# A SwiGLU layer with seven half products in place of eight in half of the inner dimension of eight chunks

## The chip, the core and the metric

The kernel runs on one core of one Trainium2 chip. The metric is the device time in microseconds (us) of one execution. The kernel is one program of three transformer blocks for 256 tokens of width 2048; the change is in the feed-forward layer of the first block.

## What is computed

Two things of the reference matter here. The feed-forward layer of the first block has 2048 inputs and 5632 hidden columns, and its result is added to the scaled input and normed:

```python
def swiglu(x, w_gu, w_d):
    gate, up = jnp.split(x @ w_gu, 2, axis=-1)
    return (jax.nn.silu(gate) * up) @ w_d

x = layer_norm(DEEPNORM_ALPHA * x + swiglu(x, ffn_wgu[l], ffn_wd[l]), ln2_g[l], ln2_b[l])
```

All weights and inputs are float32. `x` here has 256 rows, `ffn_wgu[0]` is 2048 x 11264 and `ffn_wd[0]` is 5632 x 2048.

## The kernel before

**Units.** Every large product runs over units of weights: 256 rows by 512 columns (two k-tiles of 128 rows), 128x1024 in memory. A unit goes through four engines. SyncE loads it (`unit_load`) into one of 8 raw slots. ScalarE copies it, rounded, to the high part (`unit_hi`, L217), into one of 4 split slots. VectorE subtracts the high part from the raw weights (`unit_lo`, L230) and so makes the low part in the same slot. TensorE multiplies (`block_mm`, L269 to L271): high by high, low by high and high by low, for 2 k-tiles and 2 halves of the 256 tokens, so 12 matmuls of 512 columns a unit. The counters between them are semaphores: `hi_ready`, `lo_ready` and `w_used` (TensorE has used a unit). ScalarE may write the high part of unit u only when TensorE has used unit u-4, and SyncE may load unit u only when VectorE has split unit u-8.

**Blocks.** 512 output columns for 256 tokens are a block; it takes a pair of the 8 PSUM banks (0 and 1, or 2 and 3, by turns). `evac` takes a block out of PSUM and then frees its pair (`acc_free`); TensorE waits for that before it opens the block after the next.

**The feed-forward layer** (`hidden(0)`) goes over 11 chunks of 512 hidden columns. A step of the loop has 24 units: 8 for the gate block of a chunk, 8 for its up block (all 16 k-tiles of the input), then 4 blocks of 2 units for the down product of the chunk before. After two gate units TensorE turns the hidden values of the chunk before (`turn_hidden`, eight 128x128 transposes a step into banks 4 and 5), and ScalarE and VectorE split these too. ScalarE takes the gate block out with Silu (L1855), VectorE multiplies it with the up block (L2730) and adds each down block to `x` (L1975). The first chunks and the last one are written out; the loop makes 8 trips, for chunks 2 to 9.

**The order of the work** on each engine is fixed by the code: `block_split` puts an evacuation behind the split of the second unit of the next block, so VectorE takes a block out while TensorE works on the two units of the next block, and only behind these does TensorE need the banks. GpSimd has little to do in this layer: at its start it loads vectors and, with `held_load`, four units for the next stage.

## Time and profile before

| | us |
|---|---|
| median of 3 runs | 3443.41 |
| lowest and highest of them | 3443.39, 3445.43 |
| the profiled execution | 3443.67 |
| its span, first to last instruction | 3441.9 |
| TensorE (PE) busy in the span | 3426.8 |
| VectorE (DVE) busy | 1944.3 |
| ScalarE (ACT) busy | 1609.9 |
| GpSimd (POOL) busy | 302.9 |

Some 1.8 us of the profiled execution lie outside its span. Matmuls overlap in the profile: each is shown for about 0.39 us, but the next starts 0.23 us after it. The time of TensorE is therefore read from the starts of matmuls, not from their lengths. The same holds for VectorE and ScalarE: an instruction is shown from start to end, and the next can start shortly before that end.

### The profile page before, as it was taken

The numbers are of one execution on the slowest core, as the hardware profiler recorded it, in microseconds if no ns is written. First come the engines' busy times: TensorE is split into PE (matmuls) and PEld (weight loads), VectorE is DVE, ScalarE is ACT, GpSimd is POOL, SyncE is SP. The second block draws the span as 40 slices with busy tenths as digits, with TensorE's granted clock in tenths as the row PEclk, the third lists the DMA queues.
The fourth block names the chain that finished last, engine by engine and source line by source line (L and its number), as shares of the span: only waits on it lengthen the run. The fifth ranks groups of instructions, "written<-read, shape, count | busy, mean of one in ns | idle before, by whom it ended". The sixth has DMA issues, their size and how long they took to land.

```text
span 3441.9 us, 42740 instructions
## 1 busy us (share of the span) xinstructions
PE 3426.8 (100%) x15844; PEld 2808.4 (82%) x15844; DVE 1944.3 (56%) x2315; ACT 1609.9 (47%) x2063; POOL 302.9 (9%) x418
## 2 busy tenths in 40 slices
PE   9999999999999999999999999999999999999999
PEld 8788878888888888777888878888888788888887
DVE  4544575555555755667556545567544845555546
ACT  5444444444444455454444444446556644444443
POOL 0000010000000000002343303000380000000000
PEclk9999999999999999999999999999999999999999
DMA  7555565556556455456555547655554555655554
GB/s 247 167 169 180 200 205 189 191 183 195 191 186 195 159 172 159 129 195 169 187 188 196 189 159 217 208 194 163 192 173 151 167 187 185 195 185 188 188 186 144
DMA packets 333316, 630.11 MB, mean 183 GB/s; under 512 B 33180, under 2 KB 36096, under 8 KB 331648
## 3 DMA queue, kind: packets, MB, share of 16 engines
q1 hardware_dynamic: 326272, 603.20, 54.7%
q0 software_dynamic: 6768, 25.05, 2.3%
q8 instruction: 86, 1.41, 0.2%
q14 instruction: 46, 0.38, 0.0%
q10 hardware_dynamic: 144, 0.07, 0.0%
HBM read 624.86 MB, written 2.33 MB: 182 GB/s over the span
## 4 chain that ended last, share of the span: by engine, by line
PE 97%; DVE 2%; ACT 1%; issue 0%; DVEq 0%; POOL 0%; ACTq 0%; POOLq 0%
PE psum L269 29%; PE psum L271 28%; PE psum L270 28%; PE psum L323 3%; PE psum L601 1%; PE psum L603 1%; PE psum L602 1%; PE psum L938 1%; PE psum L951 0%; PE psum L3136 0%; PE psum L519 0%; PE psum L517 0%; PE psum L518 0%; DVE weights_lo L230 0%; PE psum L3156 0%
## 5 line engine op out<-in xcount | busy, mean ns | idle before, releaser
L230 DVE TENSOR_TENSOR weights_lo<-weights_raw,weights_hi 128x1024 fp32r<-128x1024 f32 (+1 forms) x1139 | 1398.1, 1237 | 1202.5 <-ACT weights_hi L217 1201.7
L217 ACT CAST weights_hi<-weights_raw 128x1024 fp32r<-128x1024 f32 (+1 forms) x1139 | 1195.0, 1052 | 1656.1 <-PE psum L271 1644.2
L269 PE MATMUL psum<-weights_hi,act_hi 128*128 128x512 f32 x3048 | 1210.9, 397 | 0.1
L271 PE MATMUL psum<-weights_hi,act_lo 128*128 128x512 f32 x3048 | 1189.4, 390 | 0.0
L270 PE MATMUL psum<-weights_lo,act_hi 128*128 128x512 f32 x3048 | 1187.3, 390 | 0.0
L271 PEld LDWEIGHTS psum<-weights_hi,act_lo 128*128 128x128 f32 x3048 | 572.0, 188 | 122.5
L269 PEld LDWEIGHTS psum<-weights_hi,act_hi 128*128 128x128 f32 x3048 | 572.6, 188 | 121.4 <-issue 8.9
L270 PEld LDWEIGHTS psum<-weights_lo,act_hi 128*128 128x128 f32 x3048 | 573.1, 188 | 112.9
L269 PE MATMUL psum<-weights_hi,hid_hi 128*128 128x512 f32 x1320 | 517.4, 392 | 0.0
L271 PE MATMUL psum<-weights_hi,hid_lo 128*128 128x512 f32 x1320 | 514.1, 389 | 0.0
L270 PE MATMUL psum<-weights_lo,hid_hi 128*128 128x512 f32 x1320 | 513.7, 389 | 0.0
L269 PEld LDWEIGHTS psum<-weights_hi,hid_hi 128*128 128x128 f32 x1320 | 247.8, 188 | 53.1 <-issue 2.7
L271 PEld LDWEIGHTS psum<-weights_hi,hid_lo 128*128 128x128 f32 x1320 | 247.7, 188 | 52.0
L270 PEld LDWEIGHTS psum<-weights_lo,hid_hi 128*128 128x128 f32 x1320 | 247.9, 188 | 50.5
L1975 DVE TENSOR_TENSOR x<-x,psum 128x512 f32<-128x512 f32 x170 | 109.1, 683 | 103.0 <-PE psum L271 103.0
L903 POOL DMA_DIRECT2D big<-in_ffn_wgu x8 | 5.8, 724 | 1394.8 <-DVE big L2483 1024.2
L323 PE MATMUL psum<-ident,big 128*128 128x128 f32 (+1 forms) x754 | 117.3, 272 | 0.2 <-DVE hid_lo L340 0.2
L323 PEld LDWEIGHTS psum<-ident,big 128*128 128x128 f32 (+1 forms) x754 | 93.3, 139 | 28.9 <-issue 3.5
L1975 DVE TENSOR_TENSOR big<-big,psum 128x512 f32<-128x512 f32 x56 | 35.9, 683 | 54.6 <-PE psum L271 54.6
L2730 DVE TENSOR_TENSOR big<-big,psum 128x512 f32<-128x512 f32 x44 | 28.3, 685 | 64.6 <-PE psum L271 64.6
L340 DVE TENSOR_TENSOR hid_lo<-psum,hid_hi 128x512 fp32r<-128x512 f32 x76 | 52.0, 684 | 1.3 <-ACT hid_hi L332 1.3
L371 ACT COPY big<-psum 128x512 f32<-128x512 f32 (+5 forms) x113 | 50.7, 449 | 3.9 <-PE psum L3055 3.9
(452 smaller groups left out, 1934.4 us busy)
## 6 DMA issues: line engine op xcount, KB each, us to landing
weights_raw<-in_ffn_wgu SPq DMA_DIRECT2D x344, 512.0 KB, 4.3
weights_raw<-in_w_ff SPq DMA_DIRECT2D x252, 512.0 KB, 3.9
weights_raw<-in_ffn_wd SPq DMA_DIRECT2D x176, 512.0 KB, 3.6
weights_raw<-in_even_w_in SPq DMA_DIRECT2D x120, 512.0 KB, 3.5
weights_raw<-in_w_in SPq DMA_DIRECT2D x64, 512.0 KB, 3.5
weights_raw<-in_odd_w_in SPq DMA_DIRECT2D x60, 512.0 KB, 3.7
weights_raw<-in_odd_w_o SPq DMA_DIRECT2D x32, 512.0 KB, 3.6
weights_raw<-in_w_out SPq DMA_DIRECT2D x32, 512.0 KB, 3.7
```

Source lines behind the costliest of these rows:

```text
L217: nc.scalar.copy(w_hi[:, u % SPLIT_SLOTS, done:size], raw[:, u % RAW_SLOTS, done:size]).then_inc(hi_ready, 1)
L230: nc.vector.tensor_tensor(w_lo[:, u % SPLIT_SLOTS, done:size], raw[:, u % RAW_SLOTS, done:size], w_hi[:, u % SPLIT_SLOTS, done:size].bitca ...
L269: nc.tensor.matmul(o, ah, wh, start=(k + j == 0), stop=False)
L270: nc.tensor.matmul(o, ah, wl, start=False, stop=False)
L271: last = nc.tensor.matmul(o, al, wh, start=False, stop=(k + j == kts - 1))
L323: last = nc.tensor.transpose(psum[:w, 4 + t % 2, at_col:at_col + p], src, ident[:p, :p])
L340: nc.vector.tensor_tensor(dst, psum[:, 4 + t % 2, :], hi.bitcast(F32), ALU.subtract).then_inc(turn_free[t % 2], 1)
L371: nc.scalar.copy(dst, psum[:w, 4 + t % 2, :n]).then_inc(turn_free[t % 2], 1)
L601: nc.tensor.matmul(o, ah, wh, start=(u + j == 0), stop=False)
L602: nc.tensor.matmul(o, ah, wl, start=False, stop=False)
L603: last = nc.tensor.matmul(o, al, wh, start=False, stop=(2 * u + j == KT_D - 1))
L1975: return TENS(o, o, s, ALU.add)
```

## The change

For chunks 2 to 9 the half of the inner dimension in k-tiles 0 to 7 is computed by a scheme of seven products in place of eight. Token halves (2), halves of these 8 k-tiles (2) and gate or up (2) make eight products of 4 k-tiles by 128 tokens by 512 columns. The new code computes seven, P1 to P7, from sums and differences of the token halves' inputs (made once, on GpSimd, `side_sums`) and from sums of the weights (made for each chunk, on VectorE, `weight_sum`). K-tiles 8 to 15 stay as they were (gate 4 to 7 and up 4 to 7). Each P is two half units: a half unit is loaded and split like a unit (128x1024), but has 6 matmuls, not 12.

- A step has 30 splits in place of 24: 8 full gate and up units, 12 half units (P2 to P7), 8 down units, and 2 half units of P1 for the next chunk among the down units. Matmuls of 512 columns a step: 276 in place of 288.
- The weights of the scheme are loaded as quads a, b (raw slots 4 to 7) and c, d (two new buffers), among the down loads; plain units have raw slots 0 to 3. Loaded bytes are the same. Split slots stay 4, and a half unit takes a whole one.
- VectorE adds weights in place in four instructions of 128x2048 a step (for P5, P7, P6, P4), and ScalarE's high part of those units waits for the sums (`summed`).
- Partial results are taken out of banks 6 and 7: four copies on ScalarE (`snap`), and on VectorE `gate_whole` (2 instructions of 128x512), `up_whole` (3) and `hidden_whole` (2) in place of two multiplications. Silu reads SBUF.
- The last instruction of `hidden_whole` frees pair 1, for which TensorE waits before the second down block. The additions of down blocks to `x` stand behind the splits at places 26 and 28 of the step (counted from 0), and 2 and 4 of the next.
- The loop has 3 trips of two steps, with one step written out ahead and one behind.
- `evac` takes both halves of a block in one instruction, everywhere (except for Relu). Some semaphores share a name, with no further effect. `held_load` waits until the last step is nearly through, because its buffers lie where the new operands are.

The core of the diff:

```diff
+ITEMS = [("gate", 4), ("P2", 0), ("P2", 1), ("gate", 5), ("P5", 0), ("P5", 1), ("gate", 6), ("P6", 0), ("P6", 1),
+         ("gate", 7), ("P7", 0), ("P7", 1), ("up", 4), ("P4", 0), ("P4", 1), ("up", 5), ("P3", 0), ("P3", 1),
+         ("up", 6), ("up", 7)]
+DOWN = [("down", 0), ("down", 1), ("down", 2), ("down", 3), ("P1", 0), ("P1", 1),
+        ("down", 4), ("down", 5), ("down", 6), ("down", 7)]
+DOWN_LAST = [item for item in DOWN if item[0] == "down"]
+ITEM = {item: i for i, item in enumerate(ITEMS + DOWN)}
+STEP = len(ITEMS) + len(DOWN)
+SUMS = ["P5", "P7", "P6", "P4"]
+QUAD = {"a": 4, "b": 6, "c": 8, "d": 10}
+PART = {"P1": "a", "P2": "c", "P3": "d", "P4": "a", "P5": "a", "P6": "a", "P7": "b"}
...
+    quad_c, quad_d = (big(o, [P, 2, 2 * UNIT])[:, :, 0:UNIT] for o in (3072, 7168))
+    raw_at = [raw[:, i, :] for i in range(RAW_SLOTS)] + [quad[:, q, :] for quad in (quad_c, quad_d) for q in range(2)]
+    hi_at = [w_hi[:, i, :] for i in range(SPLIT_SLOTS)]
+    lo_at = [w_lo[:, i, :] for i in range(SPLIT_SLOTS)]
...
+    def high_part(act, c, of, size):
+        to = c.split_slot()
+        if to in c.user:
+            act.wait_ge(w_used, c.until(c.user[to] + 1))
...
-    def evac(eng, c, end, block, dst, do):
+    def evac(eng, c, end, block, dst, do, by_half=False):
 
 
         eng.wait_ge(w_used, c.until(end))
         pair = block % 2
-        for m in range(TT):
-            last = do(m, dst(m), psum[:, 2 * pair + m, :])
+        if by_half:
+            for m in range(TT):
+                last = do(m, dst(m), psum[:, 2 * pair + m, :])
+        else:
+            both = slice(0, TT)
+            last = do(both, dst(both), psum[:, 2 * pair:2 * pair + 2, :])
         last.then_inc(acc_free[pair], 1)
...
+            def down(ch, base, next_base):
+                quads = [(x, q) for x in "abdc" for q in range(2)] if next_base is not None else []
+                for u in range(8):
+                    if quads:
+                        quad(*quads[u], ch + 2, next_base)
+                    at = (DOWN if quads else DOWN_LAST).index(("down", u))
+                    slot_load(sp, c, c.raw_slot(), rows(w2, ch * kts + 2 * (u % 2), 2, (u // 2) * BLK), BLK, base + at)
...
+        def side_sums():
+            G = nc.gpsimd
+            halves = [(k, slice(m * P, (m + 1) * P)) for m in range(TT) for k in (slice(0, 4), slice(4, 8))]
+            for to, (k, m) in zip(token_parts, halves):
+                last = G.tensor_tensor(to[:], aT_hi[:, k, m].bitcast(F32), aT_lo[:, k, m].bitcast(F32), ALU.add)
...
+            pool.wait_ge(ready("sides_high"), 2)
+            for p in ("P5", "P6", "P7", "P3"):
+                last = G.tensor_tensor(side_lo[p][:], side_whole[p][:], side_hi[p][:].bitcast(F32), ALU.subtract)
+            last.then_inc(ready("sides_low"), 1)
...
+            def sums_item(item):
+                what, q = item
+                if what in PART:
+                    x = PART[what]
+                    slot = QUAD[x] + q
+                    if what in SUMS:
+                        act.wait_ge(ready("summed"), c.now("summed", SUMS.index(what) + 1))
+                    else:
+                        act.wait_ge(landed[slot], c.now(f"raw{slot}", 1, 1, 16))
+                        c.n[f"raw{slot}"] += 1
+                    if what == "P7":
+                        c.n[f"raw{slot}"] += 1
+                    high_part(act, c, raw_at[slot], UNIT)
+                else:
+                    unit_hi(act, c, UNIT)
...
+                    sums_item(item)
+                    if i == 0:
+                        act.wait_ge(acc_free[(start - 5) % 2], c.freed(start - 5))
+                        snap(r[:, 0, :], 6, base - 4)
+                    if i == ITEM["gate", 4] + 5:
+                        turn_taken(0)
+                    if i == ITEM["gate", 5] + 5:
+                        turn_taken(2)
+                    if i == ITEM["P5", 1] + 5:
+                        snap(up_parts[:, 1, :], 7, base + ITEM["P5", 1] + 1)
+                    if i == ITEM["P6", 1] + 4:
+                        snap(up_parts[:, 0, :], 6, base + ITEM["P6", 1] + 1)
+                    if i == ITEM["P7", 1] + 5:
+                        snap(r[:, 1, :], 6, base + ITEM["P7", 1] + 1)
+                    if i == ITEM["gate", 7] + 7:
+                        gated(0)
+                    if i == ITEM["P4", 1] + 7:
+                        gated(1)
...
+            def weight_sum(what):
+                if what == "P5":
+                    dve.wait_ge(lo_ready, c.now("unit", -1))
+                    landing("b")
+                    ins = TENS(quad_ab, quad_ab, quad_b, ALU.add)
+                elif what == "P7":
+                    dve.wait_ge(ready("summed"), c.now("summed"))
+                    landing("d")
+                    ins = TENS(quad_b, quad_b, quad_d, ALU.add)
+                else:
+                    dve.wait_ge(lo_ready, c.now("unit"))
+                    ins = TENS(quad_ab, quad_ab, quad_d if what == "P6" else quad_c, ALU.add)
+                ins.then_inc(ready("summed"), 1)
+                c.n["summed"] += 1
...
+                def gate_whole(m):
+                    dve.wait_ge(w_used, c.until(base + (ITEM["gate", 7], ITEM["P4", 1])[m] + 1))
+                    if m == 0:
+                        dve.wait_ge(ready("snapped"), c.now("snapped", 1))
+                        TENS(r[:, 0, :], bank(0), r[:, 0, :], ALU.subtract).then_inc(ready("gate_whole"), 1)
+                    else:
+                        dve.wait_ge(ready("snapped"), c.now("snapped", 4))
+                        TENS(r[:, 1, :], bank(1), r[:, 1, :], ALU.subtract).then_inc(acc_free[start % 2], 1)
+                def up_whole():
+                    dve.wait_ge(w_used, c.until(base + ITEM["up", 7] + 1))
+                    dve.wait_ge(ready("snapped"), c.now("snapped", 3))
+                    TENS(up_parts[:, 1, :], bank(2), up_parts[:, 1, :], ALU.add).then_inc(dve_step, 1)
+                    TENS(up_parts[:, 0, :], bank(7), up_parts[:, 0, :], ALU.add).then_inc(dve_step, 1)
+                    dve.wait_ge(dve_step, c.now("dve_step", 1))
+                    TENS(up_parts[:, 1, :], bank(6), up_parts[:, 1, :], ALU.add).then_inc(dve_step, 1)
+                def hidden_whole():
+                    for m in range(TT):
+                        dve.wait_ge(dve_step, c.now("dve_step", 2 + m))
+                        dve.wait_ge(ready("gated"), c.now("gated", m + 1))
+                        ins = TENS(h[:, m, :], r[:, m, :], up_parts[:, m, :], ALU.mult)
+                    ins.then_inc(acc_free[(start + 1) % 2], 1)
...
+                    if item in (("P5", 1), ("P6", 1)):
+                        weight_sum("P6" if item[0] == "P5" else "P4")
+                    if not last and i == ITEM["P1", 1] + 1:
+                        weight_sum("P5")
+                    if i == 2 and before is None:
+                        add_at(base - 2, start - 2, 2)
+                    if i == 4:
+                        if before is None:
+                            add_at(base, start - 1, 3)
+                        else:
+                            before()
+                    if i == ITEM["gate", 4] + 6:
+                        turn_taken(0)
+                    if i == ITEM["gate", 5] + 6:
+                        turn_taken(2)
+                    if i == ITEM["gate", 7] + 5:
+                        gate_whole(0)
+                    if i == ITEM["P4", 1] + 5:
+                        gate_whole(1)
+                    if i == ITEM["up", 7] + 4:
+                        up_whole()
+                    if i == ITEM["up", 7] + 5:
+                        hidden_whole()
+                    if i == ITEM["down", 1] + 5:
+                        add_at(base + ITEM["down", 1] + 1, start + 2, 0)
+                    if not last and i == ITEM["P1", 1] + 2:
+                        weight_sum("P7")
+                    if not last and i == ITEM["down", 3] + 5:
+                        add_at(base + ITEM["down", 3] + 1, start + 3, 1)
+                if last:
+                    add_at(base + ITEM["down", 3] + 1, start + 3, 1)
+                    add_at(base + len(items) - 2, start + 4, 2)
...
+            into = {"P1": 6, "P6": 6, "P7": 6, "P5": 7, "P3": 7, "P2": 0, "P4": 1}
+            behind_snap = {("P6", 0): 1, ("up", 4): 2, ("P7", 0): 3}
...
+            def sums_item(item):
+                what, q = item
+                s = c.split_slot()
+                pe.wait_ge(lo_ready, c.now("unit", 1))
+                for j in range(2):
+                    wh, wl = (w[s][:, j * BLK:(j + 1) * BLK] for w in (hi_at, lo_at))
+                    if what in into:
+                        hi, lo, k0, m = sides[what]
+                        parts = [(hi[:, k0 + 2 * q + j, m], lo[:, k0 + 2 * q + j, m], into[what])]
+                    else:
+                        parts = [(aT_hi[:, 2 * q + j, m * P:(m + 1) * P], aT_lo[:, 2 * q + j, m * P:(m + 1) * P],
+                                  ((0, 1) if what == "gate" else (7, 2))[m]) for m in range(TT)]
+                    for ah, al, b in parts:
+                        start_ = j == 0 and opens[b] == item
+                        stop = j == 1 and b in closes.get(item, ())
+                        nc.tensor.matmul(bank(b), ah, wh, start=start_, stop=False, skip_group_check=True)
+                        nc.tensor.matmul(bank(b), ah, wl, start=False, stop=False, skip_group_check=True)
+                        last = nc.tensor.matmul(bank(b), al, wh, start=False, stop=stop, skip_group_check=True)
+                last.then_inc(w_used, 1)
...
+            def sums_down(last=False):
+                pe.wait_ge(turn_free[0], c.now("turn", 1, 2))
+                pe.wait_ge(turn_free[1], c.now("turn", 0, 2))
+                for j in range(4):
+                    if j == 2 and not last:
+                        for q in range(2):
+                            sums_item(("P1", q))
+                    block_mm(pe, c, kts, BLK, hT_hi, hT_lo)
+            def sums_step(last=False):
+                start = c.n["block"]
+                for i, item in enumerate(ITEMS):
+                    if item == ("gate", 4):
+                        pe.wait_ge(acc_free[start % 2], c.freed(start - 2))
+                    if item == ("up", 4):
+                        pe.wait_ge(acc_free[(start + 1) % 2], c.freed(start - 1))
+                    if item in behind_snap:
+                        pe.wait_ge(ready("snapped"), c.now("snapped", behind_snap[item]))
+                    sums_item(item)
+                    if item == ("gate", 4):
+                        hidden_stands(start - 5, 0)
+                        turn_hidden(0)
+                    if item == ("gate", 5):
+                        turn_hidden(2)
+                c.n["block"] += 2
+                c.n["snapped"] += 4
+                sums_down(last)
```

**Where instructions stand.** First VectorE in the middle of the down product, written out ahead of the loop. `weights_lo` is the low part of a unit; `x<-x,psum` adds a down block; `big` are the gate, up and hidden values. Before, chunk 1:

```order
L2730 TENSOR_TENSOR big_196<-big_194,psum 128x512 [waits w_used,acc_free0]
L2730 TENSOR_TENSOR big_196<-big_194,psum 128x512
L230 TENSOR_TENSOR weights_lo<-weights_raw,weights_hi 128x1024 [waits hi_ready] x2
L1976 SCALAR_TENSOR_TENSOR x<-x,psum 128x512 [waits w_used]
L1976 SCALAR_TENSOR_TENSOR x<-x,psum 128x512
```

and now the first step of the scheme, from behind the split of down unit 3:

```order
L3056 TENSOR_TENSOR big_218<-psum,big_218 128x512 [waits soft_then_snapped,w_used]
L3057 TENSOR_TENSOR big_218<-psum,big_218 128x512
L3059 TENSOR_TENSOR big_218<-psum,big_218 128x512 [waits dve_step]
L301 TENSOR_TENSOR weights_lo<-weights_raw,weights_hi 128x1024 [waits hi_ready]
L3065 TENSOR_TENSOR big_198<-big_196,big_218 128x512 [waits rms_then_gated,dve_step] x2
L301 TENSOR_TENSOR weights_lo<-weights_raw,weights_hi 128x1024 [waits hi_ready] x2
L3025 TENSOR_TENSOR weights_raw<-weights_raw 128x2048 [waits unit_landed7,unit_landed6,lo_ready]
L3042 TENSOR_TENSOR x<-x,psum 128x2x512 [waits w_used]
L301 TENSOR_TENSOR weights_lo<-weights_raw,weights_hi 128x1024 [waits hi_ready]
L3029 TENSOR_TENSOR weights_raw<-weights_raw,big_60 128x2048 [waits unit_landed11,unit_landed10,end_then_summed]
```

The two multiplications that made the hidden values have become three additions, a split and two multiplications, and a sum of 128x2048 stands between a split and the addition to `x` that frees a pair of banks.

Second, VectorE at the top of a step, as the last step has it (written out, without the loop's register instructions). Before:

```order
L230 TENSOR_TENSOR weights_lo<-weights_raw,weights_hi 128x1024 [waits hi_ready] x4
L1975 TENSOR_TENSOR x<-x,psum 128x512 [waits w_used]
L1975 TENSOR_TENSOR x<-x,psum 128x512
L230 TENSOR_TENSOR weights_lo<-weights_raw,weights_hi 128x1024 [waits hi_ready] x3
L340 TENSOR_TENSOR hid_lo<-psum,hid_hi 128x512 [waits turn_hi]
```

and now:

```order
L301 TENSOR_TENSOR weights_lo<-weights_raw,weights_hi 128x1024 [waits hi_ready]
L301 TENSOR_TENSOR weights_lo<-big_59,weights_hi 128x1024 [waits hi_ready] x2
L3042 TENSOR_TENSOR x<-x,psum 128x2x512 [waits w_used]
L301 TENSOR_TENSOR weights_lo<-weights_raw,weights_hi 128x1024 [waits hi_ready] x2
L3042 TENSOR_TENSOR x<-x,psum 128x2x512 [waits w_used]
L301 TENSOR_TENSOR weights_lo<-weights_raw,weights_hi 128x1024 [waits hi_ready]
L3032 TENSOR_TENSOR weights_raw<-weights_raw,big_60 128x2048 [waits lo_ready]
L301 TENSOR_TENSOR weights_lo<-weights_raw,weights_hi 128x1024 [waits hi_ready]
L418 TENSOR_TENSOR hid_lo<-psum,hid_hi 128x512 [waits turn_hi]
```

Third, a half unit on TensorE (P1, between down units 3 and 4): one token half, so six matmuls under one wait, where a full unit before has twelve.

```order
L3651 MATMUL psum<-weights_hi,big_204 128x512 [waits lo_ready]
L3652 MATMUL psum<-weights_lo,big_204 128x512
L3653 MATMUL psum<-weights_hi,big_209 128x512
L3651 MATMUL psum<-weights_hi,big_204 128x512
L3652 MATMUL psum<-weights_lo,big_204 128x512
L3653 MATMUL psum<-weights_hi,big_209 128x512
```

Of the VectorE rows at the top of a step: the first `x<-x,psum` (down block 2, frees pair 0, which the gate block at place 0 needs) stood behind the last down split of the step before; now it stands behind the splits of places 0, 1 and 2.

## Rows read from the trace of the kernel before

**Rows 1.** The page, head and part 1: busy time of each engine.

```profile
span 3441.9 us, 42740 instructions
...
PE 3426.8 (100%) x15844; PEld 2808.4 (82%) x15844; DVE 1944.3 (56%) x2315; ACT 1609.9 (47%) x2063; POOL 302.9 (9%) x418
```

**Rows 2.** Who waited for whom, TensorE, whole span: total, times, longest.

```profile
PE psum L463 <- POOL scratch L1227: 1.1, 1, 1.1
PE psum L323 <- issue: 1.1, 1, 1.1
PE psum L323 <- DVE x L2046: 1.0, 4, 0.3
```

**Rows 3.** Windows: start-up loads, then one loop trip; busy (instructions), clock, DMA share, GB/s.

```profile
8.00:26.00 18.00, 18.00 (x89) 14.93 (x90) 10.91 (x13) 9.23 (x12) 0.00 (x0) 1.00 1.05 389
...
585.92:652.17 66.25, 66.25 (x298) 54.84 (x296) 36.23 (x36) 27.31 (x29) 0.00 (x0) 1.00 0.59 191
```

**Rows 4.** Timeline of TensorE, loop: start, length; last matmul of a unit, next unit whole.

```profile
723.92 0.39 PE L271 MATMUL psum<-weights_hi,act_lo 128*128 128x512 f32 x1
724.15 0.39 PE L269 MATMUL psum<-weights_hi,act_hi 128*128 128x512 f32 x1
...
726.87 0.39 PE L269 MATMUL psum<-weights_hi,act_hi 128*128 128x512 f32 x1
```

**Rows 5.** Timeline of ScalarE, loop: start, length, idle before and what ended it.

```profile
724.35 1.06 ACT L217 CAST weights_hi<-weights_raw 128x1024 fp32r<-128x1024 f32 x1 [1.66 <-PE psum L271]
...
732.51 1.06 ACT L217 CAST weights_hi<-weights_raw 128x1024 fp32r<-128x1024 f32 x1 [1.66 <-PE psum L271]
733.46 1.08 ACT L1855 ACTIVATE big<-psum 128x512 f32<-128x512 f32 x2
735.23 1.06 ACT L217 CAST weights_hi<-weights_raw 128x1024 fp32r<-128x1024 f32 x1 [0.69 <-PE psum L271]
```

**Rows 6.** Timeline of VectorE, loop.

```profile
704.34 1.28 DVE L1975 TENSOR_TENSOR x<-x,psum 128x512 f32<-128x512 f32 x2 [1.88 <-PE psum L271]
705.54 2.35 DVE L230 TENSOR_TENSOR weights_lo<-weights_raw,weights_hi 128x1024 fp32r<-128x1024 f32 x2
...
725.44 1.23 DVE L230 TENSOR_TENSOR weights_lo<-weights_raw,weights_hi 128x1024 fp32r<-128x1024 f32 x1 [1.37 <-ACT weights_hi L217]
```

**Rows 7.** Groups of VectorE by form, 560 to 1150 us: count, busy, mean ns.

```profile
L230 DVE TENSOR_TENSOR weights_lo<-weights_raw,weights_hi 128x1024 fp32r<-128x1024 f32 x214 | 258.9, 1223 | 186.7 <-ACT weights_hi L217 186.7
L1975 DVE TENSOR_TENSOR x<-x,psum 128x512 f32<-128x512 f32 x66 | 42.4, 683 | 44.6 <-PE psum L271 44.6
```

**Rows 8.** Timelines of VectorE and TensorE, 464 and 30 us: TensorE resumes on VectorE.

```profile
464.20 0.69 DVE L551 TENSOR_TENSOR act_lo<-psum,act_hi 128x512 fp32r<-128x512 f32 x1 [0.37 <-ACT act_hi L542]
...
464.94 0.50 PE L601 MATMUL psum<-big,act_hi 128*128 128x512 f32 x1
465.28 0.39 PE L602 MATMUL psum<-big,act_hi 128*128 128x512 f32 x1
...
29.04 2.36 DVE L230 TENSOR_TENSOR weights_lo<-weights_raw,weights_hi 128x1024 fp32r<-128x1024 f32 x2 [0.27 <-ACT weights_hi L217]
...
30.41 0.47 PE L490 MATMUL psum<-weights_hi,act_hi 128*128 128x512 f32 x1 [0.24 <-DVE weights_lo L230]
30.72 0.40 PE L491 MATMUL psum<-weights_lo,act_hi 128*128 128x512 f32 x1
```

**Rows 9.** DMA issues, 645 to 1120 us: KB each, us to landing; and queues there.

```profile
q1 hardware_dynamic: 46996, 90.60, 58.8%
q14 instruction: 1, 0.01, 0.0%
...
weights_raw<-in_ffn_wgu SPq DMA_DIRECT2D x116, 512.0 KB, 3.7
```

**Rows 10.** Groups of GpSimd by form, whole span: TENSOR_TENSOR of 128x512.

```profile
L1082 POOL TENSOR_TENSOR big<-big,big 128x512 f32<-128x512 f32 x8 | 17.3, 2158 | 0.6
```

343 lines of the change are left out of this document (292 added, 51 removed).

## The prediction

> **What bounds the kernel now.** I read the page's busy times first [rows 1]: TensorE is busy for 3426.8 of 3441.9 us, VectorE for 56% and ScalarE for 47%. Then who waited for whom: TensorE's waits are few, the longest three come to 3.2 us in the whole run [rows 2]. So TensorE is the bound everywhere, and matmuls taken away are time saved, as long as TensorE finds its operands and banks ready. Then one trip of the changed loop in windows [rows 3]: 66.25 us, TensorE never idle, VectorE busy for 36.2 and ScalarE for 27.3. Last the timelines, for what stands between one engine and the next:
>
> - A unit of 12 matmuls takes 2.72 us on TensorE (724.15 to 726.87) [rows 4], so 0.227 us a matmul and 1.36 us a half unit. 24 units are 65.3 us; the transposes take the other 0.97.
> - ScalarE starts a high part 0.20 us behind the end of the unit that frees its slot (724.15 to 724.35) [rows 4, 5]. VectorE starts the low part 1.09 us behind the high part (724.35 to 725.44) [rows 5, 6]. So a split is tied to TensorE: the low part of unit u starts 1.29 us after the end of unit u-4.
> - On VectorE two instructions of 128x512 occupy 1.20 us (704.34 to 705.54), a low part 1.14 (two end 2.35 after the start of the first, one takes 1.22) [rows 6, 7]. So 0.60 us for 512 elements, 1.14 for 1024, 0.54 for 512 more; the ends come 0.08 later.
> - TensorE starts 0.05 us behind VectorE's end (464.89 to 464.94) and its first matmul takes 0.34 us, not 0.23: 0.16 us lost. Where the wait is an instruction of its own, 0.15 (30.26 to 30.41) and a first matmul of 0.31: 0.23 us [rows 8].
>
> **What the change takes away.** 12 matmuls in each of 8 chunks: 96 x 0.227 = **21.8 us**, all on the path. The eight transposes stay.
>
> **What it adds on VectorE.** Six more splits a step (6 x 1.14), four sums of 128x2048, and five more instructions of 128x512, less what the merged `evac` saves. No row shows 128x2048: from the rows it is 1.14 + 2 x 0.54 = 2.22 us, ending at 2.3. The bounds are 2.13 (the slope alone, four times 0.54) and 2.45 (two low parts one after the other with their whole length); I take 2.21, since all rows of this form agree on the slope [rows 7]. The Trainium skill's page "VectorE: DVE Perf Modes", section "The TRN2 errata", has (N+151)/0.96 ns for a float32 tensor_tensor, an estimate of 2.29 us from start to end at 2048, with which the forecast would stay as it is; no row shows one. Altogether VectorE is occupied for about 30 x 1.14 + 4 x 2.21 + 4 x 1.14 + 9 x 0.60 = 53 us of a step of 63.5. In sum that fits. But it isn't the sum that decides: with four split slots VectorE can't work ahead by more than three units, and three half units are only 4.1 us, of which 2.5 go for the split itself. So I walk through a step. Time 0 is the start of down unit 0 (place 20) on TensorE.
>
> 1. **Second down block.** It needs the last instruction of `hidden_whole`. Low part of down 3 from 1.29 (behind up 7, which ends at 0) to 2.43; three additions to 4.23; low part of P1 to 5.37; two multiplications, the second from 5.97 to 6.65. TensorE resumes at 6.89 (0.23 behind it), and would have started at 5.44: a wait of **1.45 us**. Before, VectorE had one thing to do here and TensorE two units of time.
> 2. **Third down block.** Down 2 now ends at 9.61, so the low part of down 4 runs from 10.90 to 12.04, then the sum for P5 to 14.25, then the addition that frees the banks, ending at 15.47. TensorE could start at 15.05 (down 3, then two halves of P1), starts at 15.70: **0.65 us**.
> 3. **Fourth down block.** Low part of down 5 to 16.53, sum for P7 to 18.74, low part of down 6, addition from 19.88 to 21.10; TensorE needs it at 21.14. Hidden, with nothing to spare.
> 4. **Gate block of the next step.** Down 7, gate 4 and the first half of P2 are split by 24.4. The second half of P2 needs the slot of down 6, which ends at 23.87: its low part runs from 25.16 to 26.30, and only then comes the addition that frees pair 0, to 27.52. TensorE is through with down 7 at 26.59 and resumes at 27.76: **1.17 us**. This wait hangs on TensorE itself and doesn't go away with a faster VectorE.
> 5. **P5 to gate 7.** From 31.77 on VectorE has six low parts, an addition, two sums (each behind the end of the low part ahead, 0.13 more) and one taken transpose without a pause, and starts the low part of gate 7 at 43.90; TensorE wants it at 45.05, gets it at 45.28: **0.23 us**.
>
> Sum **3.5 us** a step, more than the 2.72 saved. Six middle steps: 21.0. The first has no wait 4 (that block is taken out ahead): 2.3. The last has no P1 between the down blocks, so wait 2 grows to 1.17: 4.0. In the first down product the addition of block 1 stands behind all splits and the sums for P5 and P7: 0.85. Together 28.2 us. In the loop a register instruction stands between such a wait and the matmul; the nearest row is the wait as an instruction of its own, 0.07 us [rows 8], with three of them in six steps 1.3 (bounds 0 and 2.6). In all **29.5 us**.
>
> **What costs nothing.** Snaps and Silu on ScalarE (30 x 0.95 + 10 x 0.5 = 34 us a step [rows 5]; the row shows that a 1.08 us piece behind a high part leaves the next on time). Six sums and copies for the sides on ScalarE in chunk 1 and the 12 instructions of 128x512 on GpSimd: at 2.16 us each [rows 10] the last four take 8.6 us, so they are done 12.8 us after TensorE's tenth unit of chunk 1, and TensorE comes to them after its sixteenth, 16.3 us on; twice that price would cost 5 us once. Loads: the same bytes, 191 GB/s before and about 188 now, where start-up shows 389 [rows 3]. Among the down units two loads of 512 KB go with each 2.72 us, 386 GB/s, but most are needed far later; the tightest is gate 4, which may be loaded from 12.3 and is wanted at 18.5, against 3.7 us to landing [rows 9]. `held_load` has some 20 units of cover. `evac` in one instruction ends 0.06 us earlier and off the path.
>
> **Sum.** 3443.7 (the profiled execution) - 21.8 + 29.5 = 3451.4; the median lies 0.3 below that execution: **3451.1 us**, 0.22% slower.
>
> **Rivals.**
> - *The waits cancel the saving.* The same mechanism with hand-overs a little cheaper: with the sum at 2.13 us, waits 1, 2 and 5 shrink and the step loses 3.0; with PE resuming in 0.16 everywhere 3.46. Waits of 15 to 28 us in all give 3436.6 to 3449.6. They decide below 28.4 us of waits, and the forecast has 29.5, so most of my error in the distances falls on this side or that of an edge that is 1 us away. 0.37.
> - *TensorE doesn't wait*: 3421.6, or up to 3436 with some waits. It needs under 1.9 us of waits a step, and waits 1 and 4 alone are 2.6; against it stands that both follow from the order and three measured distances. For it: each is built from rows of other places. 0.08.
> - *VectorE is slower in long runs.* In the walk it does 10 instructions without a pause before wait 4 and 14 around wait 5; the register instructions of the loop or PSUM reads beside matmuls could add 0.05 us to each on the path. Walking the step again with that gives 4.7 us a step, 3460; with 0.02 it is 4.1, 3455. 0.13, within "slower".
> - *The longer loop body isn't kept.* It has about 1220 instructions on TensorE, 630 before. In the loop before the instruction queues moved one packet in 475 us [rows 9], so a body of 630 stays. If this one were fetched again, the two jumps back would stall; a load takes 3.7 us to land, so up to 7 us: 3458. The Trainium skill's page "Runtime: NRT & Kernel Launch", section on instruction fetch, says a jump to a target outside the window stalls, and gives TensorE 128 KiB, 2048 instructions; by that the body fits. 0.03.
>
> **Chances and range.** Slower by over 0.2% 0.55 (forecast 0.39, the last two 0.16), within 0.2% 0.37, faster 0.08; 0.2%, 6.9 us, is about what a measurement of this kernel can tell. The likeliest case's own range is 3447 to 3456. The range for 8 in 10 takes in the cheaper hand-overs and the slower VectorE: 3441 to 3461.
>
> **What would show it.** In the profile after: 15748 matmuls; two steps take 133 to 135 us (132.5 before, 127.1 without waits); TensorE waits for VectorE's `big` (L3065) once a step for about 1.3 us, for `x` (L3042) twice, about 0.6 and 1.1; the sums (L3025 to L3032) take 2.29 us; TensorE's clock stays at its upper level. Wrong would be: waits on ScalarE or DMA of over 0.5 us a step, sums of another length, or instruction packets within the loop.

## The result, and the profile after

The changed kernel takes **3469.2 us** (median of 6 runs, 3468.4 to 3472.7), against 3443.5 for the kernel before on the same chip (6 runs, 3443.3 to 3445.4). The ratio is **1.0075**, with a 95% interval of 1.0064 to 1.0086: 0.75% slower. The forecast was 3451.1, slower by 0.22%, with 3441 to 3461 as its range. The direction is right, the size is not: 18 us are missing.

The profiled execution is the slowest of the six, 3472.7 us, which is 29.0 above the profiled one of before. Where do these 29.0 us lie? Behind the first SwiGLU layer the two traces agree to 0.1 us, ahead of it to 0.3 us. One window over the layer, of before and of after (columns as in [rows 3]: length, busy time and instructions of TensorE, of its weight loads, of VectorE, ScalarE and GpSimd, clock, DMA share, GB/s):

```profile
466.90:1202.20 735.30, 734.76 (x3288) 605.55 (x3288) 421.22 (x435) 306.67 (x320) 10.01 (x16) 1.00 0.59 192
```

```profile
466.61:1230.98 764.37, 731.72 (x3192) 589.84 (x3193) 573.59 (x510) 369.97 (x403) 30.94 (x28) 0.99 0.55 185
```

The 96 matmuls are gone (3288 to 3192), and the layer is 29.1 us longer all the same. TensorE now stands idle for 32.6 us of it (764.37 - 731.72), and its mean clock is no longer 1.00. Who it waited for, over the whole span (as [rows 2], where nothing of this layer stands):

```profile
PE psum L341 <- DVE big L3065: 14.7, 8, 4.4
PE psum L341 <- DVE weights_lo L301: 7.6, 2, 5.0
PE psum L3651 <- DVE x L3042: 6.2, 7, 0.9
PE psum L341 <- DVE x L3042: 2.5, 7, 0.9
...
PE psum L341 <- DVE x L2243: 0.9, 1, 0.9
```

The first, third and fourth line are the forecast's waits 1, 4 and 2, the last is the first down product, forecast at 0.85. The second was in no part of it: two waits, of 5.0 and 2.5 us. One stands beside GpSimd's sums, which the forecast had under "what costs nothing", the other at the first unit of the first down product. The windows by stretch show where: the layer's second chunk (two windows), its first down product, the step written out ahead, two steps of the loop, the loop's last step, the step behind the loop.

```profile
466.60:493.60 27.00, 22.22 (x102) 16.37 (x102) 22.81 (x23) 11.61 (x14) 7.17 (x7) 0.98 0.45 156
493.60:565.50 71.90, 69.14 (x296) 56.67 (x296) 37.09 (x28) 27.66 (x31) 14.89 (x8) 0.96 0.49 158
...
588.50:660.84 72.34, 69.53 (x299) 55.83 (x298) 56.07 (x49) 36.77 (x40) 0.00 (x0) 0.98 0.54 183
660.84:728.05 67.21, 64.85 (x285) 52.22 (x285) 54.05 (x47) 34.91 (x39) 0.00 (x0) 1.00 0.55 188
728.05:795.32 67.27, 64.91 (x285) 52.22 (x285) 54.04 (x47) 34.93 (x39) 0.00 (x0) 1.00 0.55 188
...
997.25:1067.21 69.96, 66.49 (x285) 53.34 (x285) 53.95 (x47) 34.81 (x39) 0.00 (x0) 0.98 0.53 180
1067.21:1140.00 72.79, 67.54 (x291) 54.81 (x292) 50.03 (x46) 33.58 (x37) 8.87 (x14) 0.98 0.59 192
```

An undisturbed step of the loop takes 67.2 us, two of them 134.5, where the forecast had 133 to 135. So the part that was walked through is right. What is missing lies at the edges: the second chunk, the first and the last steps, and in just these windows the granted clock is under 1.00.

The three waits of a step in TensorE's timeline (start, length, and in brackets the idle time with what ended it), from three stretches of the step behind 728:

```profile
728.05 0.49 PE L3651 MATMUL psum<-weights_hi,act_hi 128*128 128x512 f32 x1 [0.89 <-DVE x L3042]
```

```profile
774.23 0.49 PE L341 MATMUL psum<-weights_hi,hid_hi 128*128 128x512 f32 x1 [1.17 <-DVE big L3065]
```

```profile
783.07 0.50 PE L341 MATMUL psum<-weights_hi,hid_hi 128*128 128x512 f32 x1 [0.29 <-DVE x L3042]
```

The bracket counts from the modelled end of the last matmul, 0.39 us behind its start, where the next could have started at 0.23. The wait on the path is therefore about 0.16 more: 1.05, 1.33 and 0.46 us. The first matmul behind a wait costs another 0.1 (0.33 us, not 0.23, to the next start).

The forecast's wait 5, at gate 7, is there too, though it is too short for a bracket. VectorE's low part ends at 745.47, and TensorE starts 0.05 us behind it:

```profile
744.25 1.22 DVE L301 TENSOR_TENSOR weights_lo<-weights_raw,weights_hi 128x1024 fp32r<-128x1024 f32 x1
```

```profile
745.24 0.39 PE L3653 MATMUL psum<-weights_hi,big 128*128 128x512 f32 x1
745.52 0.50 PE L3651 MATMUL psum<-weights_hi,act_hi 128*128 128x512 f32 x1
745.86 0.40 PE L3652 MATMUL psum<-weights_lo,act_hi 128*128 128x512 f32 x1
```

The two starts, 0.29 and 0.34 us behind the ones before them, cost 0.17 us together.

The worst place of the layer's last step reads the same way, but with another number and another story on ScalarE behind it:

```profile
1116.63 0.50 PE L341 MATMUL psum<-weights_hi,hid_hi 128*128 128x512 f32 x1 [4.40 <-DVE big L3065]
...
1117.45 0.63 PE L341 MATMUL psum<-weights_hi,hid_hi 128*128 128x512 f32 x1
1117.88 0.63 PE L342 MATMUL psum<-weights_lo,hid_hi 128*128 128x512 f32 x1
```

```profile
1104.16 1.05 ACT L282 CAST weights_hi<-weights_raw 128x1024 fp32r<-128x1024 f32 x1 [0.85 <-DMA weights_raw<-in_ffn_wd]
1110.13 1.05 ACT L282 CAST weights_hi<-weights_raw 128x1024 fp32r<-128x1024 f32 x1 [4.92 <-DMA weights_raw<-in_ffn_wd]
```

ScalarE waits 4.92 us for the load of the fourth down unit; on VectorE the sums of the up product and the hidden activations are queued behind that unit's low part, so TensorE waits for them. And from 1117.45 on the starts are 0.43 us apart and no longer 0.23: the clock is at half, 1.2 in place of 2.4 GHz. The granted clock in short windows behind five waits (5.4, 2.2, 1.6, 2.8 and 4.8 us from matmul to matmul):

```profile
493.99:500.00 6.01, 6.01 (x15) 4.75 (x16) 6.01 (x3) 0.46 (x1) 5.85 (x4) 0.54 0.62 196
638.40:642.00 3.60, 3.60 (x11) 2.85 (x12) 1.00 (x1) 0.00 (x0) 0.00 (x0) 0.65 0.72 266
706.99:711.00 4.01, 4.01 (x18) 3.30 (x19) 1.16 (x1) 0.95 (x1) 0.00 (x0) 1.00 0.70 258
1044.61:1049.00 4.39, 4.39 (x13) 3.44 (x14) 1.01 (x1) 0.00 (x0) 0.00 (x0) 0.62 0.43 160
1116.63:1121.00 4.37, 4.37 (x12) 3.46 (x13) 1.08 (x1) 0.00 (x0) 0.00 (x0) 0.61 1.05 388
```

Behind the wait of 1.6 us the clock stays; behind the four others it is at half, by the trace's clock record for 6.8 us and three times 3.4. Of the 6.8 us, 1.25 lie ahead of 493.99, where TensorE still stood, so 15.8 us at half were felt, and they cost 7.9.

The sum for the profiled run, each wait counted from matmul start to matmul start less the usual 0.227: 5.2 and 2.7 ahead of the steps, 1.1 in the first down product; third down units (hidden activations) 16.0; third down blocks 3.7; gate blocks 7.4; half clock 7.9. Together 44.0. With 0.1 us behind each of some 22 waits (2.2) and 0.3 us a step in small places (wait 5 the largest of them; 2.6), less the 21.8 saved, that gives 27.0 of the 29.1. (The expectation of x9_all below counts the clock with all 17.1 us, as 8.5.)

### The profile page after: what moved, and what is told of

The parts are those of the page before. It is cut to its first block, busy times and chain, and to the rows that moved or that the text cites. A ratio compares the mean times of both kernels' runs of the same rounds, so it can differ in the third digit from the quotient of the medians.

```text
span 3470.7 us, 42634 instructions
## 1 busy us (share of the span) xinstructions
PE 3422.7 (99%) x15748; PEld 2791.9 (80%) x15748; DVE 2091.4 (60%) x2299; ACT 1670.9 (48%) x2135; POOL 323.0 (9%) x430
## 4 chain that ended last, share of the span: by engine, by line
PE 91%; DVE 4%; ACT 2%; issue 2%; DMA 1%; SPq 0%; DVEq 0%; ACTq 0%
PE psum L341 24%; PE psum L343 24%; PE psum L342 24%; PE psum L401 3%; PE psum L3651 3%; PE psum L3653 3%; PE psum L3652 3%; DVE weights_lo L301 1%; ACT weights_hi L282 1%; DMA weights_raw<-in_ffn_wd 1%; PE psum L681 1%; PE psum L1030 1%; PE psum L683 1%; PE psum L682 1%; DVE x L3042 1%
## 5 line engine op out<-in xcount | busy, mean ns | idle before, releaser
L301 DVE TENSOR_TENSOR weights_lo<-weights_raw,weights_hi 128x1024 fp32r<-128x1024 f32 (+1 forms) x1155 | 1428.2, 1247 | 1135.0 <-ACT weights_hi L282 1132.7
L282 ACT CAST weights_hi<-weights_raw 128x1024 fp32r<-128x1024 f32 (+1 forms) x1155 | 1207.8, 1049 | 1586.1 <-PE psum L343 1437.6
L341 PE MATMUL psum<-weights_hi,act_hi 128*128 128x512 f32 x2536 | 1011.4, 399 | 5.1 <-DVE weights_lo L301 5.0
L343 PE MATMUL psum<-weights_hi,act_lo 128*128 128x512 f32 x2536 | 990.9, 391 | 0.0
L342 PE MATMUL psum<-weights_lo,act_hi 128*128 128x512 f32 x2536 | 989.0, 390 | 0.0
L341 PEld LDWEIGHTS psum<-weights_hi,act_hi 128*128 128x128 f32 x2536 | 477.2, 188 | 107.6 <-issue 14.4
L343 PEld LDWEIGHTS psum<-weights_hi,act_lo 128*128 128x128 f32 x2536 | 476.6, 188 | 102.5
L342 PEld LDWEIGHTS psum<-weights_lo,act_hi 128*128 128x128 f32 x2536 | 477.7, 188 | 93.3
L3651 PE MATMUL psum<-weights_hi,act_hi 128*128 128x512 f32 x320 | 127.1, 397 | 6.2 <-DVE x L3042 6.2
L3653 PE MATMUL psum<-weights_hi,act_lo 128*128 128x512 f32 x320 | 124.8, 390 | 0.0
L3652 PE MATMUL psum<-weights_lo,act_hi 128*128 128x512 f32 x320 | 124.7, 390 | 0.0
L2242 DVE TENSOR_TENSOR x<-x,psum 128x1024 f32<-128x1024 f32 x54 | 65.8, 1219 | 60.4 <-PE psum L343 60.4
L3651 PEld LDWEIGHTS psum<-weights_hi,act_hi 128*128 128x128 f32 x320 | 60.1, 188 | 23.6 <-issue 7.9
```

The lines of the kernel that those rows point to most:

```text
L282: nc.scalar.copy(hi_at[to][:, done:size], of[:, done:size]).then_inc(hi_ready, 1)
L301: nc.vector.tensor_tensor(lo_at[to][:, done:size], of[:, done:size], hi_at[to][:, done:size].bitcast(F32), ALU.subtract).then_inc(lo_ready, 1)
L341: nc.tensor.matmul(o, ah, wh, start=(k + j == 0), stop=False)
L342: nc.tensor.matmul(o, ah, wl, start=False, stop=False)
L343: last = nc.tensor.matmul(o, al, wh, start=False, stop=(k + j == kts - 1))
L2242: return TENS(o, o, s, ALU.add)
```

## The experiments

Theory after the comparison: the loss is a sum of separate delays, three from the order in which VectorE takes its work, and three at the edges: GpSimd's side sums, loads, and GpSimd's early loads for the next stage. The rival: VectorE has no room, and what is taken from one wait turns up at the next. Differences below are medians against the changed kernel's 3469.2; the kernel before, run beside each experiment, had medians of 3443.5 to 3443.8. Most experiments have four runs, which lie 2 to 9 us apart. So a difference of about 4 us (x3_add0, x6_held, x4_loads, x8_ring) isn't clear of the scatter: the ranges of those four meet the changed kernel's. There the trace has to show what went or came.

**VectorE's order, one line at a time.** The three edits, in this order x1_gate, x2_hidden and x3_add0 (x11_order has all three):

```diff
-                    if i == 2 and before is None:
+                    if i == 1 and before is None:
                         add_at(base - 2, start - 2, 2)
...
-                    if i == ITEM["up", 7] + 4:
+                    if i == ITEM["up", 7] + 3:
                         up_whole()
-                    if i == ITEM["up", 7] + 5:
+                    if i == ITEM["up", 7] + 3:
                         hidden_whole()
...
-                    if i == ITEM["down", 1] + 5:
+                    if i == ITEM["down", 1] + 4:
                         add_at(base + ITEM["down", 1] + 1, start + 2, 0)
```

> The changed kernel with one line of VectorE's order changed: in the steps of seven half-unit products, the addition of the third block of the down product into x stands behind the split of place 1 and no longer behind that of place 2. Theory (the addition comes one unit too late, so that the gate block waits): the wait of 1.28 us (1.05 over the usual gap of 0.23) in front of TensorE's gate block, seven times in the profile of the changed kernel, goes, and the wait in front of the next place does not appear; 7 x 1.05 = 7.4 us less: 3461.9 us against 3469.2. Rival (the gate block is as late as what VectorE has to do in the stretch, so the wait only moves to the splits of places 1 and 2): no change, 3469 +- 2.

Measured: 3463.7 us (3460.5 to 3464.7), -5.5 of the 7.4 expected. The waits of L3651 for L3042 are gone from the list, and nothing came in their place:

```profile
PE psum L341 <- DVE big L3065: 15.3, 8, 4.5
PE psum L341 <- DVE weights_lo L301: 7.6, 2, 5.0
PE psum L341 <- DVE x L3042: 2.8, 8, 0.8
```

> The changed kernel with VectorE's sums of the up product (L3056 to L3059) and the product that makes the hidden activations (L3065) both moved to behind the split of place 22, from behind 23 and 24; nothing else. Theory of the order (they stand behind splits that themselves wait for TensorE and for the load of the fourth down unit): all eight waits of the third down unit in L341 (2.18, 1.56 four times, 1.86, 2.78, 4.79 us, in sum 16.0 over the usual gaps) go, the load being needed only one unit later; with them go the three stretches at half clock behind the longest of them (3 x 1.7 = 5.1 us): about 3448 us. Rival (the late loads alone make them): what goes is only the 1.33 us a step that the splits cost, seven times, 9.3 us, and in the first and the last step the wait stands at the fourth down unit instead: 3460.

Measured: 3451.4 us (3450.8 to 3453.6), -17.8 of the 21 expected. All eight waits for L3065 are gone, in the last step too, although there ScalarE still waits 4.93 us for the same load:

```profile
1095.20 1.05 ACT L282 CAST weights_hi<-weights_raw 128x1024 fp32r<-128x1024 f32 x1 [4.93 <-DMA weights_raw<-in_ffn_wd]
```

So the late load was not enough for the wait: it needed the sums queued behind it. With the sums ahead, TensorE wants that load one unit later. A wait of 1.76 us, 1.5 over the usual gap, is left at the third down block of the last step. The half clock behind the hidden waits is gone as well; only the stretch at 494 us is left.

> The changed kernel with one line of VectorE's order changed: the addition of the first down block stands behind the split of place 25, and no longer behind that of place 26 and the weight sum for P5. Theory (the third down block waits 0.69 us because the addition stands behind that sum): this wait, 0.46 us over the usual gap eight times and 1.0 in the last step, goes: -3 to -4 us, 3465.8 against 3469.2. Rival (the sum, now behind the addition, makes its own split late): a wait of about the same length at P1 or at the fifth down unit, 3469.

Measured: 3465.1 us (3461.3 to 3470.5), -4.2. The waits at the third down block are gone. For all three edits the waits went where the theory had them, and none as long came in their place.

> The changed kernel with the three changes of VectorE's order alone (x1_gate, x2_hidden and x3_add0 together): SyncE's loads, GpSimd's sums, the split ring as in the changed kernel. Theory (these waits are separate, each made by the order in which VectorE takes its work): the steps go at TensorE's pace and the sum of the three is given back, 5.5 + 17.8 + 3.5 = 26.8 us: 3442.4, level with the kernel before. Rival (they share VectorE's free time, the splits become late in their place): 3447 to 3452, and the rest of x9_all's 38.6 us is not explained by the side sums (6.1) and the next stage's loads (3.7).

Measured: **3437.0 us** (3436.0 to 3438.3), ratio to the kernel before 0.9981 (0.9971 to 0.9990), -32.2, where the three alone give 27.5. TensorE's waits for VectorE in this layer are now the two at the low parts (7.6 us, ahead of the steps) and one of 0.7 in the first down product; in the steps there is none but the 0.17 us of wait 5. That is 4.7 us better than the sum of the three; the long waits act on the clock as well, and that part need not add up line by line, though no run takes the two apart. Three moves turn the change from 0.75% slower to 0.19% faster.

**GpSimd beside VectorE.** VectorE and GpSimd at the start of the second chunk, changed kernel:

```profile
487.07 6.77 DVE L301 TENSOR_TENSOR weights_lo<-weights_raw,weights_hi 128x1024 fp32r<-128x1024 f32 x1
```

```profile
487.80 4.95 POOL L1388 TENSOR_TENSOR big<-act_hi,act_lo 128x512 f32<-128x512 f32 x4
492.83 2.14 POOL L1392 TENSOR_TENSOR big<-big,big 128x512 f32<-128x512 f32 x1
```

A low part that takes 1.23 us elsewhere takes 6.77, until GpSimd's fourth sum is done; the next ones take about 2.3 beside sums of 2.1 to 2.3, which take 1.25 each while VectorE stands. TensorE runs out of split units:

```profile
493.99 0.76 PE L341 MATMUL psum<-weights_hi,act_hi 128*128 128x512 f32 x1 [5.02 <-DVE weights_lo L301]
```

> The changed kernel with the twelve sums and low parts of the activations' sides (128x512 each) taken from GpSimd and given to VectorE, one or two behind each split of the layer's second chunk; no GpSimd arithmetic is left there. Theory (GpSimd and VectorE held each other up at 487 to 494 us: a low part took 6.77 us and TensorE waited 5.41 us, then ran 6.8 us at half clock): both go, 5.2 + 3.4 = 8.6 us less: 3460.6. Rival (the wait at 494 us belongs to the start of the layer, whoever does the sums): within 2 us of 3469; and if VectorE has no room there, the wait stands elsewhere in the same chunk.

The core of the edit (GpSimd's `side_sums` is left out, and its twelve instructions go to VectorE, through the hook that runs behind each split u of the chunk):

```diff
-            side_sums()
...
+                def side_sums(u):
+                    if u < 4:
+                        k, m = slice(4 * (u % 2), 4 * (u % 2) + 4), slice((u // 2) * P, (u // 2 + 1) * P)
+                        tied(TENS(token_parts[u][:], aT_hi[:, k, m].bitcast(F32), aT_lo[:, k, m].bitcast(F32), ALU.add))
+                    elif u < 7:
...
-                after = step(1, after, True, at_down=down)
+                after = step(1, after, True, also=side_sums, at_down=down)
```

Measured: 3463.1 us (3461.6 to 3464.4), -6.1. The wait at 494 us and the half clock behind it are gone; the layer's second chunk has no wait at all.

> The changed kernel in which GpSimd makes the first four of its twelve side sums (128x512 each) twice, with the same result; nothing else. Theory (each of them holds VectorE up by about as long as it runs on GpSimd, 1.26 us, since one low part of VectorE took 6.77 us beside four of them): a second low part of some 6 us beside the second four, TensorE waits longer by 2.5 to 5 us at 494 us, where its cover of three split units is used up already: 3473 to 3475. Rival (the low part was held up by something else, and the sums only stand beside it): 3469 +- 2.

```diff
-            for to, (k, m) in zip(token_parts, halves):
-                last = G.tensor_tensor(to[:], aT_hi[:, k, m].bitcast(F32), aT_lo[:, k, m].bitcast(F32), ALU.add)
-            pool_link(pc, last)
+            for again in range(2):
+                for to, (k, m) in zip(token_parts, halves):
+                    last = G.tensor_tensor(to[:], aT_hi[:, k, m].bitcast(F32), aT_lo[:, k, m].bitcast(F32), ALU.add)
+                pool_link(pc, last)
```

Measured: 3470.1 us (3468.7 to 3473.2), +0.9: no difference that can be told. My expectation is refuted. The first low part again took 6.79 us, but the four sums more then took turns with low parts, and those have enough cover (TensorE waits nowhere else in that chunk):

```profile
487.16 6.79 DVE L301 TENSOR_TENSOR weights_lo<-weights_raw,weights_hi 128x1024 fp32r<-128x1024 f32 x1
```

```profile
487.16 15.67 DVE L301 TENSOR_TENSOR weights_lo<-weights_raw,weights_hi 128x1024 fp32r<-128x1024 f32 x5
```

Five low parts in 15.67 us, the first included: 2.2 us each for the other four. What costs is the first meeting, not the amount. The last experiment takes the meetings away and leaves the amount:

> The changed kernel in which each of GpSimd's first eight side sums waits for one low part of VectorE to end (the 155th to the 162nd of the kernel, from 505 us on), so that it runs in the 1.5 us before VectorE's next one; the same sums on the same engine. The four behind ScalarE's copies stay. Theory (what costs is that a sum of GpSimd and an instruction of VectorE stand beside each other, the first of which took 6.77 us; x7_twice shows that how many sums there are doesn't matter): TensorE's wait of 5.4 us at 494 us and the half clock behind it go as in x5_side, low parts take 1.23 us: 3460.6 to 3463.5 against 3469.2. Rival (GpSimd's sums cost VectorE their own length wherever they stand): low parts from 505 us on take 2 us or more; with TensorE's cover of three units that shows as no wait at all, so the low parts, not the time, tell the two apart.

```diff
-            for to, (k, m) in zip(token_parts, halves):
+            for n, (to, (k, m)) in enumerate(zip(token_parts, halves)):
+                pool.wait_ge(lo_ready, 155 + n)
                 last = G.tensor_tensor(to[:], aT_hi[:, k, m].bitcast(F32), aT_lo[:, k, m].bitcast(F32), ALU.add)
             pool_link(pc, last)
...
+            pool.wait_ge(lo_ready, 159)
             G.tensor_tensor(s3, a21, a11, ALU.subtract)
```

(and so for the next three, 160 to 162.) Measured: 3463.1 us (3462.1 to 3465.3), -6.1, the same as with no sums on GpSimd. Both engines have their short times, VectorE over the stretch from 490 to 530 us and GpSimd in one place of it:

```profile
L301 DVE TENSOR_TENSOR weights_lo<-weights_raw,weights_hi 128x1024 fp32r<-128x1024 f32 x16 | 19.5, 1225 | 19.2 <-ACT weights_hi L282 19.2
```

```profile
499.71 1.29 POOL L1389 TENSOR_TENSOR big<-act_hi,act_lo 128x512 f32<-128x512 f32 x1 [1.43 <-DVE weights_lo L301]
```

So the two engines slow each other only while both have an instruction under way. The Trainium skill has this rule, in "SBUF — State Buffer", section "Who interferes with whom": a VectorE instruction with two SBUF inputs and a GpSimd instruction that reads SBUF share a port pair, and whichever starts first has it for its whole length. The turns of 2.3 us agree with it: a low part's 1.14 and a sum's 1.25 are 2.4. The first meeting does not: the low part began first (487.07, the sum 487.80), and yet it was the low part that stood, for the length of four sums. It ended 1.09 us behind the fourth sum (492.75 to 493.84), so almost its whole length was still to do by then. All nine kernels that leave these sums on GpSimd ungated show this low part at 6.77 to 6.79 us. It isn't GpSimd's issue of a load at 487.14, which stands there too: in x12_between the same issue, at 487.25, lies beside low parts of 1.22 and 1.23. Why the low part stood, and why the later ones took turns, no run here tells; experiments on the order of the two starts weren't made.

**The next stage's loads.**

> The changed kernel in which GpSimd's loads for the next stage (four quads of 512 KB and the vectors behind them) wait until VectorE has split the last step's eighth down unit, and no longer start in the middle of its up product; nothing else. Theory (in the last step the load of the fourth down unit lands 9.05 us after its issue at 1101.06 because these loads run beside it, ScalarE waits for it until 1110.1, and the sums of the up product stand behind it): the wait of 4.79 us at 1116.6 shrinks to about the 1.56 us of the other steps, the 3.4 us at half clock behind it go: -3.2 - 1.7 = -4.9, 3464.3 us against 3469.2. Rival (the order of VectorE alone makes it): the wait stays at 4 us or more, 3469. A cost of the move would be seen at the start of the next stage, at 1231 us.

```diff
-            pool.wait_ge(lo_ready, sums_from["unit"] + ITEM["P3", 1] + 1)
+            pool.wait_ge(lo_ready, sums_from["unit"] + len(ITEMS) + 8)
```

Measured: 3465.5 us (3463.2 to 3469.7), -3.7. In the last step ScalarE no longer waits for the load, and TensorE's wait for the hidden activations is 1.53 us from start to start, as in a quiet step, where it was 4.79:

```profile
1102.23 1.05 ACT L282 CAST weights_hi<-weights_raw 128x1024 fp32r<-128x1024 f32 x1 [1.67 <-PE psum L3653]
```

Behind the layer the trace is as long as the changed kernel's (2239.7 us both), so the move costs the next stage nothing. Together with x2_hidden this settles the last step: the early loads made the fourth down unit late, the order handed that on to TensorE, and either edit alone is enough to break it.

**The order of the loads, and a ring that is set back.**

> The changed kernel with another order of SyncE's loads in the down stretch: the quads of side a between the first two down units, both of b ahead of the third, those of d behind the fourth, those of c behind the fifth; in the very first down product the four down units go ahead of all quads. Nothing else. Theory (where a step's wait at the third down unit is over 1.56 us, the load of the fourth down unit was late, landing 6.4 to 9 us after its issue behind quads): steps one, six, seven and last lose 0.6 + 0.3 + 1.2 + part of 3.2 us, the first down product its gap of 2.9 us, and the half-clock stretches behind 2.18 and 2.78 us go; the 1.56 us of the other steps stay. About 3469.2 - 2.7 - 2.1 - 3.4 - 1 = 3460. Rival (the loads are not what is waited for; the order of VectorE is all of it): 3469 +- 2. A third: moving them only moves the crowding, and the sums of weights wait for the quads: slower than 3469.

```diff
-                quads = [(x, q) for x in "abdc" for q in range(2)] if next_base is not None else []
-                for u in range(8):
-                    if quads:
-                        quad(*quads[u], ch + 2, next_base)
+                order = list(range(8))
+                if next_base is not None:
+                    order = ([0, 1, 2, 3, "a0", "a1", "b0", "b1", "d0", "d1", 4, 5, "c0", "c1", 6, 7] if first else
+                             ["a0", 0, "a1", 1, "b0", "b1", 2, 3, "d0", "d1", 4, "c0", "c1", 5, 6, 7])
```

Measured: 3473.8 us (3471.4 to 3476.4), +4.5: nearest to the third of the expectations. In two steps of the loop, quieter in the changed kernel, ScalarE waited for the same down unit and TensorE for 2.4 to 2.7 us.

```profile
834.66 1.05 ACT L282 CAST weights_hi<-weights_raw 128x1024 fp32r<-128x1024 f32 x1 [2.82 <-DMA weights_raw<-in_ffn_wd]
```

That the new order moved the crowding there isn't shown. x7_twice, whose loads are those of the changed kernel, has such a wait in the loop as well, with 2.85 us on TensorE behind it at 910.92:

```profile
904.34 1.05 ACT L282 CAST weights_hi<-weights_raw 128x1024 fp32r<-128x1024 f32 x1 [2.96 <-DMA weights_raw<-in_ffn_wd]
```

So the step in which this load is late changes without a change of the loads, and the traced run of x4_loads (3471.4) even lies below the traced one of the changed kernel (3472.7).

More telling is what didn't change. In the first down product the loads of the first four down units now landed early (by 556.7 us), and yet ScalarE stood for 9.82 us there, as in the changed kernel, and it is TensorE that it waits for:

```profile
563.22 1.04 ACT L282 CAST weights_hi<-weights_raw 128x1024 fp32r<-128x1024 f32 x1 [9.82 <-PE psum L343]
```

```profile
562.79 3.89 ACT L282 CAST weights_hi<-weights_raw 128x1024 fp32r<-128x1024 f32 x4 [9.82 <-PE psum L343]
```

Why for TensorE, with four split slots? Because the code sets the ring of split slots back to slot 0 here, and 173 units have been split by then: 173 is one over a multiple of four, so slot 0 holds the unit split last. ScalarE must wait until TensorE is through with everything, and then TensorE stands for the split of a unit (high and low part, 2.3 us).

> The changed kernel in which the ring of the four split slots is not set back to slot 0 where the layer's sums begin and end, but goes on from where it stands; nothing else. 173 units are split before that place, so slot 0 there is the slot of the unit split last, and ScalarE has to wait for TensorE to finish with it. Theory (this drain of the ring is the wait of 2.93 us at TensorE's first down unit, 565.67 us, and ScalarE's idle time of 9.8 us in front of it; x4_loads left both as they were with its loads landed 6 us earlier): the wait goes or shrinks to below 0.6: -2.7 us, 3466.5. Rival (SyncE's burst of eight loads makes it): the second down unit comes late in place of the first, 3469 +- 1.

```diff
-                    c.rings(range(4), range(SPLIT_SLOTS))
+                    c.rings(range(4))
...
-                c.rings(None, range(SPLIT_SLOTS))
+                pass
```

(on all three engines.) Measured: 3473.2 us (3471.3 to 3477.5), +3.9. Neither theory had it all. ScalarE no longer waits for TensorE there, but now for the load, which the burst of eight makes late, and one wait became three of 0.8 to 2.4 us over the usual gap:

```profile
560.28 1.05 ACT L282 CAST weights_hi<-weights_raw 128x1024 fp32r<-128x1024 f32 x1 [8.32 <-DMA weights_raw<-in_ffn_wd]
```

The two causes lie one behind the other. To tell, both have to go, and the other waits with them:

> The changed kernel with all of these together: the addition of the third down block behind place 1, the sums of up and the hidden activations behind place 22, the addition of the first down block behind place 25 (ahead of the sum for P5), the sides' sums on VectorE, GpSimd's loads for the next stage behind the last step's down splits, the split ring running on. Theory (the time over the saved products is the sum of separate waits and of the half clock behind the long ones): 7.4 at the gate blocks, 16.0 at the third down units, 3.7 at the third down blocks, 5.2 + 2.7 + 1.1 ahead of the steps, 8.5 for the clock are given back, 44.6 us: about 3425, faster than the kernel before by 0.5%. Rival (VectorE has no room in the step: what is taken from one wait turns up at the next): 3435 to 3445.

Measured: 3430.7 us (3428.6 to 3430.9), ratio 0.9960 (0.9946 to 0.9975). That is 5.7 us over the theory and 4.3 under the rival's range. In the steps no wait is left but wait 5, so VectorE does have the room; the three waits of x8_ring in the first down product remain (the longest, for the addition that frees the banks, is 2.2 us in the list of waits), with 3.4 us at half clock behind them.

> As x9_all, with the order of loads of x4_loads as well. Theory (with the split ring running on, the first down product can use its down units as soon as they have landed, and the quads of b are there for the sum of P5): 0 to 2 us below x9_all, at the first down product. Rival (x4_loads was slower by 0 to 4 us because its order brings quads closer to the plain loads): 0 to 4 us above x9_all, with waits at places where a down unit or a sum waits for its load.

Measured: **3425.0 us** (3424.7 to 3426.7), ratio **0.9945 (0.9928 to 0.9962)**, 18.5 us faster than the kernel before and 44.3 faster than the changed one. Now the high parts follow TensorE through the first down product one by one:

```profile
552.65 1.05 ACT L282 CAST weights_hi<-weights_raw 128x1024 fp32r<-128x1024 f32 x1 [1.67 <-PE psum L343]
555.37 1.05 ACT L282 CAST weights_hi<-weights_raw 128x1024 fp32r<-128x1024 f32 x1 [1.67 <-PE psum L343]
```

By the medians the loads' order alone cost 4.5 us and the ring alone 3.9, neither clear of the scatter; on top of the rest, ring included, the order gives 5.7, and that is clear (3424.7 to 3426.7 against 3428.6 to 3430.9). The ring and the order without the other edits weren't run together. The layer, and one step of it:

```profile
466.69:1183.53 716.84, 715.92 (x3192) 587.04 (x3193) 569.97 (x522) 370.30 (x403) 10.33 (x16) 1.00 0.58 197
708.12:771.97 63.85, 63.85 (x285) 52.53 (x284) 54.03 (x47) 34.96 (x38) 0.00 (x0) 1.00 0.58 198
```

The layer is 18.5 us shorter than before, the saving of 21.8 less 3.3: one wait of 0.6 at 574.8 us, and about 0.3 a step. The step takes 63.85 us; 66.25 less twelve matmuls is 63.53. Of the 0.32 us between them 0.17 is wait 5 again: the low part of gate 7 ends at 725.41 and TensorE starts at 725.47, 0.28 us after its last start, and takes 0.34 to the next. The rest is spread over the step in pieces of under 0.02.

```profile
724.19 1.22 DVE L301 TENSOR_TENSOR weights_lo<-weights_raw,weights_hi 128x1024 fp32r<-128x1024 f32 x1
```

```profile
725.18 0.39 PE L3684 MATMUL psum<-weights_hi,big 128*128 128x512 f32 x1
725.47 0.50 PE L3682 MATMUL psum<-weights_hi,act_hi 128*128 128x512 f32 x1
```

A wait that is met already, such as those for the snaps, costs nothing that can be read: apart from these places and those behind the transposes, which the kernel before has too, every start in the step comes at most 0.24 us after the last.

## Why the prediction was wrong

The step that failed is "What costs nothing", together with the sign that "TensorE's clock stays at its upper level". The sum had 29.5 us of delays and the profiled run has 50.9 (29.1 longer, with 21.8 saved). Of the missing 21.4 us four terms that the sum had at nothing make up 21.1: GpSimd's sums beside VectorE (5.2), the first down unit (2.7), the late load of the fourth down unit in four steps (5.3) and the half clock (7.9). The walk through a quiet step, from which most of the sum came, held.

- **The saving, 21.8 us**: right. x10_all_loads gives 18.5 of it back in the layer. The missing 3.3 are one wait of 0.6 and 0.3 a step, of which 0.17 is the forecast's wait 5.
- **Length of the sums**: taken as 2.21 us of occupied time ending at 2.3; measured 2.28 to 2.29 from start to end. Right.
- **The walk through a step, 3.5 us**: right place by place, and its sum a little by luck. Forecast 1.45, 0.65, 1.17 and 0.23; measured 1.33, 0.46 and 1.05, with 0.1 behind each, and 0.17. The fourth down block, "hidden, with nothing to spare", wasn't quite hidden: its first starts are 0.27 and 0.33 us behind the last (721.43 and the next), 0.14 us. A quiet step took 67.2 us against 63.53 without waits: 3.7. x1_gate, x2_hidden and x3_add0 show that each of the first three is made by where VectorE's order has the work that TensorE waits for.
- **Register instructions, 1.3 us**: not there. The wait at the gate block is 1.28 or 1.29 us from start to start in the loop and 1.25 in the last step, which is written out: at most 0.04 each, where the forecast had 0.07.
- **"This wait hangs on TensorE itself"** (wait 4): true for the order as written, but it didn't hang on TensorE beyond that. One place earlier the addition had all that it needed, and the wait was gone.
- **First and last step, 2.3 and 4.0 us**: wrong. The first had 3.4 us at half clock and a late load (6.4 us from issue to landing); in the last the wait for the hidden activations alone was 4.6. What failed here is "`held_load` has some 20 units of cover". That counted when its data are needed, not what the traffic does to the loads beside it. [rows 9] had 3.7 us to landing; in the last step the fourth down unit took 9 us from issue to landing.
- **"Loads: the tightest is gate 4"**: wrong. The tightest is the fourth down unit. In a quiet step it landed 0.3 us before ScalarE wanted it (700.09 against 700.41), since the quads share the queue: the median from issue to landing of the down units in the loop is 6.4 us in the trace of after, 3.5 in that of before. In two steps of the loop it came later than that, and TensorE's wait was 1.86 and 2.78 us where a quiet step has 1.56; why in those two, no run tells. I had noted the 386 GB/s among the down units next to the 389 at start-up [rows 3] and drawn nothing from it.
- **GpSimd's sums "at 2.16 us each"**: [rows 10] has the length of a sum on GpSimd, and I priced GpSimd's own path with it. That a sum of 2.16 us had perhaps been slowed by VectorE, and so VectorE by it, I didn't ask, although the rule on the shared port pair, named above, speaks to it. It cost 5.2 us of waiting and 2.8 for the clock in the profiled run (x5_side and x12_between: 6.1 in the median).
- **First down product, 0.85 us**: 1.1 at the place that I meant. The 2.7 at its first unit I hadn't seen: it stands in the code (`rings`) and needs a count of units mod four.
- **The clock**: forecast to stay at its upper level. It fell at four waits, 7.9 us. This is the largest term of the error, and no walk through the order gives it.
- **The longer loop body isn't kept**: refuted. "Instruction packets within the loop" was a sign of it, and from 645 to 1060 us there are nine; but all lie ahead of the second trip (the last at 769.7 us), and from 795 to 1060 there is none. So the body is fetched once and kept. No wait stands at the jumps, and x10_all_loads runs the steps at 63.83 to 63.89 us each. The Trainium skill's figure for TensorE in "Runtime: NRT & Kernel Launch", section "Instruction fetch mechanics", by which a body of this length fits, agrees with that.
- **VectorE slower in long runs**: refuted; low parts take 1220 ns in the steps of after, 1223 before [rows 7].

Of the 18 us missing in the median, the second chunk (5.2), the first down unit (2.7), the hidden activations in the four steps where they took more than 1.56 (5.3 more) and the half clock (7.9) are 21.1 in the profiled run, which is itself 3.5 us above the median. How much falls to the clock varies from run to run (below), so the terms can't be fixed to better than some 3 us.

## What to carry to other kernels

When an in-order engine gets more work, its sum of busy time says little: write down for each instruction when its input is there and who waits for its output, and move it to the first place where it needn't wait. Three such moves were worth 32 us here, more than the whole saving. And price an edge by its neighbours: a load by what it delays, an instruction on GpSimd by what it does to VectorE, a ring that is set back by which slot comes next.

When one cause is removed and nothing changes, as with the loads and with the ring, there may be a second one right behind it: only in x10_all_loads, where both are gone (and the other waits too), is the wait gone.

## What the runs showed of the hardware

- **GpSimd and VectorE hold each other up.** Alone 1.23 us (128x1024 on VectorE) and 1.29 us (128x512 on GpSimd); with both under way about 2.3 and 2.1 to 2.3; once, at the first meeting, 6.77 to 6.79 us for the one on VectorE, through four sums of 1.25, in each of the nine kernels that have it. Placed between each other's instructions they cost nothing (x12_between). The 2.16 us in [rows 10] was not GpSimd's own speed: each of the eight lies beside VectorE instructions for 1.0 to 1.9 us.
- **TensorE's clock falls to half (1.2 GHz) at short waits.** In these thirteen traces, in this layer, it never fell at a wait of up to 2.13 us from start to start, fell to half at some of those from 2.2 to 3.0 (at 2.93, the same instruction, it did in x1_gate, x4_loads and x12_between and did not in the changed kernel and six others), and always at 4.75 to 5.45, there often before TensorE was back at work. It stayed at half for 3.4 or 6.8 us. The runs of one kernel with such waits lie 2.3 (x11_order) to 9.2 us (x3_add0) apart, those of x10_all_loads 1.9. That the clock makes this scatter fits, but isn't shown: only one run of each kernel has a trace.
- **One stretch at half clock is left open.** In x10_all_loads, x11_order and x12_between 3.4 us at half clock stand in a later stage (1417 us in x10_all_loads), where TensorE's longest gaps are under 0.8 us and the same as in the kernel before, whose clock stayed up in its profiled run. It costs 1.7 us, and the traced run of x10_all_loads lies 1.6 to 1.9 above its three others. The windows show it, and nothing here says why:

```profile
1412.00:1416.00 4.00, 4.00 (x29) 3.39 (x28) 1.95 (x7) 1.05 (x1) 0.00 (x0) 1.00 0.38 131
1416.00:1421.00 5.00, 5.00 (x18) 3.71 (x15) 1.96 (x7) 0.00 (x0) 0.00 (x0) 0.66 0.29 105
```

- **Loads near the limit wait for each other.** Where loads of 512 KB are issued faster than one in 1.35 us, they land 1.35 us apart, at some 390 GB/s, and each one's time to landing grows by what is queued: 3.3 to 3.5 us alone, 4.4 to 8.8 in a quiet step's down stretch, and up to 14 in the last step, behind GpSimd's loads.
